# Half of the gate tables written by indirect accumulating transfers instead of by one-hot products

## The reference, cut to what matters

```
top_s, top_i = lax.top_k(scores, 16)              # per head and half
cand_s = top_s[..., 0, :, None] + top_s[..., 1, None, :]
best_s, best_pos = lax.top_k(cand_s, 16)
best_i = ...                                      # first key * 128 + second key
gate = jax.nn.softmax(best_s, axis=-1)            # 8 heads x 16 gates a token
act = gelu(x . expert_u[best_i])
y   = sum over k of gate * act * expert_v[best_i]
```

## Time and profile before

| | |
|---|---|
| median of 3 runs | 1366.83 us (1365.65 to 1368.29) |
| span of the profiled execution | 1367.0 us |
| TensorE busy | 1339.9 us (98%) |
| VectorE busy | 1004.8 us (74%) |
| ScalarE busy | 650.3 us (48%) |
| GpSimd busy | 104.6 us (8%) |
| mean granted TensorE clock | 0.996 |

### The profile page before, as it was taken

How to read it: one execution, slowest core, us unless ns; L and a number is a source line. 1 busy time by engine, 2 the same in 40 slices (tenths; PEclk the granted TensorE clock), 3 DMA queues, 4 the chain that set the end, 5 groups by cost and what they waited for, 6 DMA issues and landing times.

```text
span 1367.0 us, 17820 instructions
## 1 busy us (share of the span) xinstructions
PE 1339.9 (98%) x7206; PEld 1143.1 (84%) x7206; DVE 1004.8 (74%) x1593; ACT 650.3 (48%) x610; POOL 104.6 (8%) x140
## 2 busy tenths in 40 slices
PE   8999999999999999999999999999989999999998
PEld 6888778888788887988888899999878888888887
DVE  6547668888465876689989899999556666666664
ACT  5455553334445455455565554544544444444441
POOL 0101200000020000000000010010110000100000
PEclk9999999999999999999999999999999999999999
DMA  9324279997352215557776667877968788878860
GB/s 364 141 102 154 99 278 353 378 370 307 132 188 105 93 62 192 173 188 240 236 235 216 211 222 240 282 254 241 347 240 336 288 289 285 287 295 290 297 243 31
DMA packets 113361, 317.27 MB, mean 232 GB/s; under 512 B 7169, under 2 KB 73985, under 8 KB 91649
## 3 DMA queue, kind: packets, MB, share of 16 engines
q1 hardware_dynamic: 95232, 249.03, 51.2%
q0 software_dynamic: 18048, 67.12, 13.8%
HBM read 281.51 MB, written 34.60 MB: 231 GB/s over the span
## 4 chain that ended last, share of the span: by engine, by line
PE 89%; DVE 5%; ACT 3%; DMA 1%; issue 1%; POOL 0%; SPq 0%; ACTq 0%; DVEq 0%; POOLq 0%
PE psum L482 87%; PE psum L485 2%; DVE slab_lo L1627 2%; DMA hidden_store<-arena 1%; ACT arena L1314 0%; POOL statistics L435 0%; ACT slab_hi L1208 0%; DVE residual L1699 0%; DMA ident<-in_ident 0%; ACT arena L1231 0%; DVE arena L2002 0%; ACT arena L1351 0%; ACT arena L1211 0%; DVE arena L1650 0%; DVE residual L2295 0%
## 5 line engine op out<-in xcount | busy, mean ns | idle before, releaser
L1627 DVE TENSOR_TENSOR slab_lo<-slab_raw,slab_hi 128x2048 fp32r<-128x2048 f32 x206 | 469.5, 2287 | 174.7 <-ACT slab_hi L1208 174.4
L1208 ACT ACTIVATE slab_hi<-slab_raw 128x2048 fp32r<-128x2048 f32 x206 | 392.3, 1910 | 234.5 <-PE psum L482 234.5
L482 PE MATMUL psum<-slab_hi,x_parts 128*128 128x512 f32 x1536 | 493.6, 395 | 5.0 <-ACT x_parts L1240 1.7
L482 PE MATMUL psum<-x_parts,slab_hi 128*128 128x512 f32 (+1 forms) x1344 | 424.8, 373 | 6.0 <-DVE arena L2101 5.0
L482 PEld LDWEIGHTS psum<-slab_hi,x_parts 128*128 128x128 f32 x1536 | 288.5, 188 | 68.3 <-ACT x_parts L1240 4.5
L482 PE MATMUL psum<-x_parts,slab_lo 128*128 128x256 f32 x1184 | 333.2, 281 | 0.0
L482 PE MATMUL psum<-slab_lo,x_parts 128*128 128x512 f32 x768 | 300.5, 391 | 0.0
L482 PEld LDWEIGHTS psum<-x_parts,slab_hi 128*128 128x128 f32 x1344 | 243.4, 190 | 53.1 <-DVE arena L2101 6.0
L482 PEld LDWEIGHTS psum<-x_parts,slab_lo 128*128 128x128 f32 x1184 | 225.3, 190 | 0.0
L482 PEld LDWEIGHTS psum<-slab_lo,x_parts 128*128 128x128 f32 x768 | 144.4, 188 | 28.3 <-issue 0.5
L482 PE MATMUL psum<-slab_hi,weighted_hi 128*128 128x512 f32 x296 | 116.2, 393 | 0.4 <-DVE residual L1699 0.4
(11 more groups left out here) (253 smaller groups left out, 1193.4 us busy)
## 6 DMA issues: line engine op xcount, KB each, us to landing
slab_raw<-in_ex_u SPq DMA_DIRECT2D x128, 512.0 KB, 5.3
slab_raw<-in_ex_v SPq DMA_DIRECT2D x64, 1024.0 KB, 5.5
arena<-in_w_ada SPq DMA_DIRECT2D x24, 1024.0 KB, 6.9
slab_raw<-in_w_gu SPq DMA_DIRECT2D x22, 1024.0 KB, 7.2
slab_raw<-in_w_in SPq DMA_DIRECT2D x21, 1024.0 KB, 5.4
hidden_store<-arena POOLq DMA_DIRECT2D x32, 512.0 KB, 4.8
gates_store<-arena POOLq DMA_DIRECT2D x8, 2048.0 KB, 13.2
arena<-hidden_store POOLq DMA_DIRECT2D x32, 512.0 KB, 5.4
```

Of the source, the lines that this page charges most:

```text
L482: return PE.matmul(out, lhsT, rhs, start=start, stop=stop)
L1208: ACTE.activation(slab_hi[:, slot, :], raw[:, slot, :], ACT.Copy).then_inc(hi_made[slot], 1)
L1627: DVE.tensor_tensor(slab_lo[:, slot, :], raw[:, slot, :], slab_hi[:, slot, :].bitcast(f32), ALU.subtract).then_inc(lo_made[slot], 1)
```

## The change

- The first 128 tokens (`tb` = 0, one token a partition) no longer go through one-hot products. There are 16 groups instead of 32, for tokens 128 to 255, one in each of the steps 32 to 47. The transposes and copies of `selection` take only these tokens.
- For the first 128 tokens, VectorE computes the place of each gate in `gates_store` (`gate_at`), in 6 small operations before `places` and 6 after the second keys.
- GpSimd first fills that half of `gates_store` with zeros, by 32 transfers of 256 KB (`clear_gates`): four after each of the first three query copies, and twenty after the last one.
- GpSimd then issues 128 indirect transfers (`scatter_gates`), six in each turn from s = 33 to 53 and two in turn 54. Each takes one gate from each of the 128 partitions and adds it at that partition's place in HBM. Before the first of each head (every 16 transfers) GpSimd waits until all earlier ones have landed. It waits for all 128 at `LAST_HIT`.
- Four blocks of 2 MB are stored instead of eight.

```diff
-NSTEP = S // 8
+NSTEP = P // 8
+GATE_K = P // GATE_T
-    return min(NSTEP, max(0, (s - GATE_FROM + 1) * 4 // 3))
+    return min(NSTEP, max(0, s - GATE_FROM + 1))
...
+            POOL.memset(sel_g[:], 0.0).then_inc(sem("gate_zeros_set"), 1)
...
+            def clear_gates(c):
+
+                POOL.dma_start(gates_store[c, :, 0:GATE_K, :].rearrange("p k n -> p (k n)").rearrange("p (j n) -> p j n", n=S),
+                               sel_g[:].unsqueeze(1).to_broadcast([P, 2, S])).then_inc(sem("gates_cleared"), 16)
+
+            POOL.wait_ge(*after("gate_zeros_set", 1))
+            for c in range(EX_N):
+                if c % 4 == 0:
+                    POOL.wait_ge(*after("query_copied", min(c // 4 + 1, 4)))
+                clear_gates(c)
+
+            def scatter_gates(j):
+
+                if j == 0:
+                    POOL.wait_ge(*after("gates_cleared", 16 * EX_N))
+                    POOL.wait_ge(*after("gate_places_made", 1))
+                elif j % TOPK == 0:
+                    POOL.wait_ge(*after("gates_scattered", 16 * j))
+                POOL.indirect_dma_start(gates_flat, bass.IndirectOffsetOnAxis(ap=gate_at[:, j:j + 1], axis=0),
+                                        gate_value[:, j:j + 1], None, compute_op=ALU.add).then_inc(
+                    sem("gates_scattered"), 16)
...
+            scattered = lambda s: min(SEL, max(0, 6 * (s - GATE_FROM)))
             for s in range(2 * EX_N):
                 c, late = divmod(s - LAG, 2)
                 if s >= LAG and not late:
                     store_hidden(c)
-                for block in range(S // GATE_T):
+                for block in range(GATE_K):
                     if s == gates_end(block) + 1:
                         store_gates(block)
+                for j in range(scattered(s - 1), scattered(s)):
+                    scatter_gates(j)
                 if s == LAST_HIT:
                     for k in range(2):
-                        POOL.wait_ge(*after(f"gates_stored{k}", 16 * (S // GATE_T // 2)))
+                        POOL.wait_ge(*after(f"gates_stored{k}", 16 * (GATE_K // 2)))
+                    POOL.wait_ge(*after("gates_scattered", 16 * SEL))
...
-                for tb in range(TB):
-                    ins = tr(ps[:, bank, tb * P:tb * P + P], src[:, tb, :])
-                ins.then_inc(sem(name + "_transposed"), 1)
+                tr(ps[:, bank, 0:P], src[:, 1, :]).then_inc(sem(name + "_transposed"), 1)
...
+            place, low_a = carve(11264 + 2 * SEL, SEL), carve(11264 + 3 * SEL, SEL)
+            V(DVE.tensor_copy(gate_value, sg_[:, 0, :]))
+            V(DVE.tensor_copy(gate_at, sa[:, 0, :]))
+            V(DVE.tensor_scalar(place, sbb[:, 0, :], float(GATE_T * S // GATE_T * EX_A), token_at, ALU.mult, ALU.add))
+            V.after()
+            V(DVE.tensor_scalar(gate_at, gate_at, EX_A - 1, None, ALU.bitwise_and))
+            V.after()
+            V(DVE.tensor_copy(low_a, gate_at))
+            V.after()
+            V(DVE.scalar_tensor_tensor(place, low_a, float(GATE_T - P * S), place, ALU.mult, ALU.add))
+            V.after()
+            DVE.scalar_tensor_tensor(gate_at, sa[:, 0, :], float(P * S), place, ALU.mult, ALU.add).then_inc(
+                sem("gate_places_made"), 1)
```

More of the change, by code:

```diff
@@ L152 @@
                           ("second_keys_made_transposed", 1)),
-    "choice_made": (("gate_softmax_made", 1), ("first_keys_made", 1), ("second_keys_made", 1)),
+    "choice_made": (("gate_softmax_made", 1), ("first_keys_made", 1), ("second_keys_made", 1), ("gate_places_made", 1)),
+    "pool_filled": (("gate_zeros_set", 1), ("half_set", 1), ("ada_cleared", 3), ("ml_rows_cleared", 1)),
+    "gates_written": (("gates_cleared", 16 * EX_N), ("gates_scattered", 16 * SEL)),
 }
@@ L326, in program @@
         gates_store = nc.dram_tensor("gates_store", (EX_N, P, S // GATE_T, EX_A * GATE_T), f32).ap()
+        gates_flat = gates_store.rearrange("c p k n -> (c p k n)").unsqueeze(1)
+        gate_at = carve(11264, SEL).bitcast(u32)
+        gate_value = carve(11264 + SEL, SEL)
+        token_at = cols[:, 200:201]
         g2, g2_diag, g2_y = carve(0, D), carve(1024, KT, P), carve(2048, TB, D)
@@ L445, in store_gates @@
                 POOL.wait_ge(*after("gates_copied", (block + 1) * (GATE_T // 8)))
-                POOL.dma_start(gates_store[:, :, block, :].rearrange("c p n -> p c n"),
+                POOL.dma_start(gates_store[:, :, GATE_K + block, :].rearrange("c p n -> p c n"),
                                gates_out[block % 2].rearrange("p (c a) t -> p c (a t)", a=EX_A)).then_inc(
@@ L1599, in scalar_program @@
                         ACTE.wait_ge(*after(name + "_transposed", 1))
-                        ACTE.activation(dst[:], ps[:, bank, 0:S], ACT.Copy).then_inc(sem("choice_copied"), 1)
+                        ACTE.activation(dst[:, 0:P], ps[:, bank, 0:P], ACT.Copy).then_inc(sem("choice_copied"), 1)
                 for i in range(gates_due(s - 1), gates_due(s)):
@@ L2172, in vector_program @@
             choose(3)
+            index = carve(12800, P)
+            V(DVE.tensor_tensor(index, ident[:], iota[:], ALU.mult))
+            V.after()
+            V(DVE.tensor_reduce(token_at, index, AX.X, ALU.add))
+            V.after()
+            V(DVE.tensor_copy(U(cols[:, 201:202]), token_at))
+            V.after()
+            V(DVE.tensor_scalar(U(cols[:, 201:202]), U(cols[:, 201:202]), 5, None, ALU.logical_shift_right))
+            V.after()
+            V(DVE.tensor_copy(cols[:, 202:203], U(cols[:, 201:202])))
+            V.after()
+            V(DVE.scalar_tensor_tensor(token_at, cols[:, 202:203], float(GATE_T * EX_A - GATE_T), token_at, ALU.mult, ALU.add))
             places = lambda n: carve(10240 + n * TB * SEL, TB, PEER_H, TOPK)
@@ L2285, in vector_program @@
                     for k in range(2):
-                        DVE.wait_ge(*after(f"gates_stored{k}", 16 * (S // GATE_T // 2)))
+                        DVE.wait_ge(*after(f"gates_stored{k}", 16 * (GATE_K // 2)))
                     gate_diagonal(5, g2_diag).then_inc(sem("gate2_diagonal_made"), 1)
```

## The result

The changed kernel takes 1464.59 us (median of 4 runs, 1463.04 to 1465.56) against 1367.56 for the kernel before: a ratio of 1.071 [1.0695, 1.0725]. It is 7.1% slower; 1341.5 us was forecast. Its profiled execution has a span of 1461.7 us, 94.7 us more than before.

What follows compares the result with a forecast made beforehand. TensorE was taken to bound the kernel: 28.1 us of removed work, less 6.6 of lateness behind GpSimd's queue, plus 4 from the stall, gives 25.5 off 1367.0, so 1341.5 us. The range, leaving 2 in 10 out, was 1331 to 1388.

Steps and rivals of the forecast that it cites:

- the price t of a scatter: GpSimd's time for one of 128 indirect transfers, taken as 1.00 us, between bounds of 0.53 and 1.80.
- the choice among the cases: Forecast with t from 0.95 to 1.12 given 0.43; all hidden 0.15; GpSimd too slow 0.21; other slower cases 0.09 and 0.05.
- plain transfer plus reading a column: How t was priced on GpSimd: 0.53 plus 0.58 less 0.11 for a bare memset, 1.00 us.
- The formula around t: TensorE's lateness from turn 55's chunk store behind GpSimd's queue: 128 t - 121.4 us, if positive; 6.6 us at 1.00.
- What was removed: On TensorE, sixteen groups at 1.74 us (27.8) and three selection transposes (0.3): 28.1 us together.
- the covers given to the clearing and to VectorE: Clearing transfers and VectorE's twelve small operations, hidden in spare or idle time: no cost; some 3 us each if not.
- The stall: Near 994 us TensorE waits 4.4 us for chunk 28's store, plus 2.9 at low clock; 4 of 7.3 expected back.
- GpSimd paces the stage: Rival: above t = 1.17 each further tenth costs 12.8 us; at t = 1.3, 1384 us; chance 0.21.
- The rival with t = 1.80: Rival: GpSimd scatters at the upper price, TensorE 109 us late, 1448 us; chance 0.05.
- reads one by one: Rival's reason: a scatter reads its places by small commands, about 102 cycles each, not pipelined; 1448 us, chance 0.05.
- Held-up VectorE: Rival: scatters hold VectorE up, 0.5 us each making it 37 us late, about 1376 us; chance 0.09.

Runs made afterwards that it cites:

- plain_write: The changed kernel with plain indirect writes instead of accumulating ones, keeping one gate where two heads chose the same expert: 1403.96 us, ratio 1.0261.
- no_scatter: The changed kernel without its 128 scatters, so the gates of the first 128 tokens stay zero: 1334.65 us, ratio 0.9762.
- before_ runs: The kernel before with chunk stores on ScalarE's queue, with two chunks' loads two turns later, or with both: 1359.84, 1359.77 and 1361.4 us.
- The probe: The kernel before plus 56 GpSimd transfers after the result, eight of each kind; for 128 rows, adding took 1.54 us and plain 0.96 us each.
- half_slow: The changed kernel with scatters of only four of the eight heads, three in a turn instead of six: 1350.42 us, ratio 0.9872.
- act_store: The changed kernel with the chunk stores issued from ScalarE's queue instead of GpSimd's: 1427.82 us, ratio 1.0436.

## Why the prediction was wrong

The step that failed is the price t of a scatter, taken as 1.00 us, and so the choice among the cases. With its pause a scatter held GpSimd's queue for (219.7 + 36.8) / 128 = 2.00 us, twice as long.

- **t = 1.00 us.** The term was mis-sized. GpSimd's scatters span 782.97 to 1069.00 us. In 286.0 us there are 128 x 1.54 = 197.1 of bare scatters, 22.6 by which VectorE lengthens them (219.7 - 197.1), 36.8 of pauses, 16.5 of waits, and 13.0 that are left for the 14 stores. (Their own records sum to more, since a store behind a scatter begins before the scatter's record ends, as at 1068.45.) The forecast had 128 + 21 + 13. Of the 124 us more, 69 are the bare scatter, 37 the pauses, 23 VectorE; the waits were 4.5 too high. The price "plain transfer plus reading a column" was nearly that of a *plain* indirect write (0.96); no run shows that it is made of these two parts, so the match may be luck. What it left out: the addition (0.58), the pause between two of them (0.30), and the time lost beside VectorE's subtractions (0.18). The pause has no row in the trace before; plain transfers follow each other without one.
- **The formula around t was right.** With the measured start of turn 55's store the lag is 1068.45 - 934.3 - 5.1 = 129.0 us; 129.0 - 28.1 - 7.3 = 93.6 us slower, against 94.7 in the spans. The same formula gives plain_write's span within about 2 us: its scatters would end near 783 + 153.5 + 36.9 + 20.8 + 13 = 1007, so 1007 - 939.4 - 35.4 = 32.4 us slower, against 1401.5 - 1367.0 = 34.5.
- **What was removed** was right within some 2 us, and so were the covers given to the clearing and to VectorE: with the stall, no_scatter gained 36.4 us in spans and 33.3 in medians, against 28.1 + 7.3.
- **The stall** went wholly in no_scatter, where I had taken 4 of its 7.3 us. By itself it is worth 6.6 to 6.9 us in the medians of the three before_ runs.
- **The rival "GpSimd paces the stage"** is what happened, with its place right and its example (t = 1.3) too low. The range ended at t = 1.33. The rival with t = 1.80, given 0.05, has the nearest time (1448), but by luck: its reason, reads one by one, is not what the rows show. The Trainium skill's rule (GPSIMD Engine Reference, Performance pitfalls for Q7 kernels) that one read per index costs about 102 cycles would show as a cost by rows. The probe has 0.21 us between 32 and 128 rows.
- **"Held-up VectorE"** was right that the two engines meet, and wrong on who pays. VectorE's comparisons grow by 0.04 to 0.10 us in the mean (780 to 966 us, against the kernel before), within what it has to spare, and its subtractions stay at 2.28. GpSimd loses 22.6 us, in the queue that decides.

## What to carry to other kernels

Price an instruction that the trace does not show by its parts: the plain form, what the option adds, the pause to the next one, and what it meets on other engines; and let the range go up to where all parts are dear. Before filling an idle engine, count what else stands in its fixed queue: GpSimd was 92% idle here, yet its 8% held the stores that TensorE waits for two steps later. Divide the time between two such deadlines by the price: 14.8 us / 2.1 us is 7 scatters before stores and waits are taken off, and 12 were issued. With six, half_slow still lost 15.8 us.

## What the hardware showed that I had not expected

- An accumulating indirect transfer occupies GpSimd for 1.54 us, a plain one for 0.96, both followed by 0.30 us before the next. The number of rows hardly matters (1.33 us for 32).
- A scatter that begins while VectorE subtracts two 128 x 2048 tiles in SBUF ends about 1.4 us after the subtraction does, so that single ones took up to 3.47 us; beside one-operand comparisons it stays at 1.54.
- With pauses in every two steps the mean granted clock of TensorE is 0.77 to 0.86 of full speed from 800 to 1050 us, and TensorE is busy 21.5 us longer than in no_scatter. With one long pause (act_store) the mean over the span is nearly the same, 0.966 against 0.961, but the low clock falls where nothing runs: TensorE is busy for 1310.0 us, 2.4 more than in no_scatter. A mean clock over the span does not tell what the clock cost.
